# First and sixth Strassen product as one 512-column and one 256-column matmul

## What is computed

```python
def conv_ffn(h, w_up, w_conv, b_conv, w_down):          # first block
    g, v = jnp.split(h @ w_up, 2, axis=-1)              # 1024 -> 2 x 2816
    g = depthwise_conv_seq(g, w_conv, b_conv)           # three taps over the tokens
    return (jax.nn.silu(g) * v) @ w_down
...
proj = h @ w_in[l]                                      # second block, 1024 -> nine parts
xc, gb, gc, q, k, v, g_sw, gate_a, gate_r = jnp.split(proj, split_points, axis=-1)
...
x = x + (jax.nn.silu(h2 @ w_ff_gate[l]) * (h2 @ w_ff_up[l])) @ w_ff_down[l]
```

## Time and profile before

| | us |
|---|---|
| median of 3 runs (1523.29 to 1524.03) | 1523.39 |
| span of the profiled execution, first to last instruction | 1521.2 |
| median over that span | 2.2 |
| PE busy in the span | 1497.1 (98%) |
| DVE busy | 1046.6 (69%) |
| POOL busy | 1013.0 (67%) |
| ACT busy | 635.8 (42%) |

### The profile page before, as it was taken

One profiled execution on the slowest core, in us unless ns is written; L12 is line 12 of the kernel. 1 busy time (PEld: TensorE's weight loads), 2 busy tenths in 40 slices (PEclk: granted clock), 3 DMA queues, 4 the chain that ended last, 5 costly groups with the idle time before them and its releaser, 6 DMA issues.

```text
span 1521.2 us, 26964 instructions
## 1 busy us (share of the span) xinstructions
PE 1497.1 (98%) x9391; PEld 1355.7 (89%) x9391; DVE 1046.6 (69%) x1605; ACT 635.8 (42%) x1142; POOL 1013.0 (67%) x801
## 2 busy tenths in 40 slices
PE   7999999999999999999999999999999999999998
PEld 6998999998887899999888888888888999999897
DVE  7877777873428477766943667676457787777954
ACT  6543566650113355565122213232235565554442
POOL 4735877766666777776764647566466787776684
PEclk9999999999999999999999999999999999999998
DMA  9942333344233333445342232322232333333342
GB/s 374 404 154 73 102 104 97 101 153 160 97 111 87 94 112 116 121 126 152 96 123 69 84 109 83 118 74 83 70 97 84 97 111 103 103 110 87 95 114 69
DMA packets 236382, 179.30 MB, mean 118 GB/s; under 512 B 5393, under 2 KB 214673, under 8 KB 235921
## 3 DMA queue, kind: packets, MB, share of 16 engines
q1 hardware_dynamic: 235008, 171.98, 36.5%
q10 hardware_dynamic: 1296, 6.29, 1.2%
HBM read 173.01 MB, written 5.24 MB: 117 GB/s over the span
## 4 chain that ended last, share of the span: by engine, by line
PE 57%; DVE 5%; issue 3%; POOL 2%; ACT 1%; POOLq 0%; DVEq 0%; ACTq 0%
PE ps L1075 19%; PE ps L1078 19%; PE ps L1079 19%; POOL tmp L929 1%; POOL w_lo L947 0%; POOL tmp L938 0%; POOL rope_r L947 0%; DVE wide_lo L3130 0%; DVE ps L3116 0%; DVE act_lo L3124 0%; DVE ps L3117 0%; DVE ps L3118 0%; DVE tmp L3115 0%; PE ps L1509 0%; DVE gates_r L3124 0%
## 5 line engine op out<-in xcount | busy, mean ns | idle before, releaser
L1075 PE MATMUL ps<-act_hi,w_hi 128*128 128x256 f32 (+1 forms) x864 | 283.6, 328 | 3.0 <-ACT gates L1895 1.3
L915 POOL TENSOR_TENSOR w_lo<-raw,w_hi 128x1024 fp32r<-128x1024 f32 x110 | 274.7, 2497 | 9.2
L1078 PE MATMUL ps<-act_hi,w_lo 128*128 128x256 f32 (+1 forms) x864 | 280.1, 324 | 0.0
L1079 PE MATMUL ps<-act_lo,w_hi 128*128 128x256 f32 (+1 forms) x864 | 280.0, 324 | 0.0
L1075 PE MATMUL ps<-wide_hi,w_hi 128*128 128x512 f32 (+2 forms) x733 | 261.1, 356 | 1.5 <-POOL w_lo L915 0.6
L1078 PE MATMUL ps<-wide_hi,w_lo 128*128 128x512 f32 (+2 forms) x733 | 260.4, 355 | 0.0
L1079 PE MATMUL ps<-wide_lo,w_hi 128*128 128x512 f32 (+2 forms) x733 | 260.4, 355 | 0.0
L912 POOL TENSOR_TENSOR w_hi<-raw,zero 128x1 fp32r<-128x1 f32 x110 | 30.3, 275 | 260.7 <-PE ps L1075 259.8
L947 POOL TENSOR_TENSOR w_lo<-raw,w_hi 128x512 fp32r<-128x512 f32 x128 | 165.8, 1305 | 52.5 <-ACT w_hi L1643 51.9
L1075 PEld LDWEIGHTS ps<-act_hi,w_hi 128*128 128x128 f32 x864 | 165.1, 191 | 19.6 <-issue 3.2
L1078 PEld LDWEIGHTS ps<-act_hi,w_lo 128*128 128x128 f32 x864 | 165.2, 191 | 13.9 <-issue 1.4
(11 more groups left out here) (322 smaller groups left out, 3952.8 us busy)
## 6 DMA issues: line engine op xcount, KB each, us to landing
raw<-in_w_in SPq DMA_DIRECT2D x88, 512.0 KB, 4.2
gates<-in_w_mod_t SPq DMA_DIRECT2D x20, 1024.0 KB, 10.2
raw<-in_w_ffn_up SPq DMA_DIRECT2D x40, 512.0 KB, 3.9
raw<-in_w_ffn_down SPq DMA_DIRECT2D x22, 512.0 KB, 3.6
raw<-in_w_ff_gate SPq DMA_DIRECT2D x22, 512.0 KB, 3.8
raw<-in_w_ff_up SPq DMA_DIRECT2D x22, 512.0 KB, 3.8
raw<-in_w_r_out SPq DMA_DIRECT2D x16, 512.0 KB, 3.4
raw<-in_w_ff_down SPq DMA_DIRECT2D x16, 512.0 KB, 3.8
```

Of the source, the lines that this page charges most:

```text
L915: nc.gpsimd.tensor_tensor(w_lo[:, two, :], raw[:, slot, :], f32(w_hi[:, two, :]), SUB).then_inc(split_done, 1)
L1075: ins = mm(o, w, a, start=start, stop=False)
L1078: mm(o, wl, a, start=False, stop=False)
L1079: return mm(o, w, al, start=False, stop=stop)
```

## The change

F1 and F6 are computed with two matmuls for each of their four feature blocks, in place of three. The first streams 512 columns past the high weights: the 256 columns of the high activations and, from another place of the same tensor, the 256 columns of the low ones. It writes a whole PSUM bank: the high part's result in the low half, the low part's in the high half. The second streams the high activations past the low weights, into the low half. DVE adds the two halves: a new join `q` adds Q1's high half to `part_q1`, `u` then takes Q6's low half, and a new last step takes away Q6's high half. `joined` now counts six steps in a pair (`q`, a step that counts as `p`, `u`, `vw`, `c1`, `c2`), each of the first two followed by a wait of DVE for itself. PE's F1 waits besides for the earlier pair's `q`. High and low activations are laid out as one tensor so that one access pattern reaches both; the sizes are as before.

```diff
--- before.py
+++ after.py
@@ -123,7 +123,7 @@
 HI = {"first": ("copy", F5, F7, F2, F1, F6, F3, F4), "later": ("copy", F1, F6, F7, F5, F2, F3, F4)}
 LO_POOL = {"first": (F7, F2, F5, F1, F4), "later": (F1, F7, F2, F4)}
 LO_DVE = {"first": ("add6", F6, "add3", F3), "later": ("add6", F6, F5, "add3", F3)}
-JOINED = ("u", "vw", "c1", "c2")
+JOINED = ("q", "p", "u", "vw", "c1", "c2")
 
 
 DOWN_PAIRS = 4
@@ -213,7 +213,7 @@
 
 def down_joined(f, j, what):
 
-    at = {"u": 1, "w": 2, "v": 3, "x": 4, "c1": 6, "c2": 8}
+    at = {"u": 1, "w": 2, "v": 3, "x": 4, "c1": 8, "c2": 12}
     return LOADED + (BASE[3 + f] + PAIR * (j - 1)) * len(JOINED) + at[what]
 
 
@@ -257,13 +257,12 @@
         res = sb("res", [P, KT, T])
         with nc.sbuf_tensor("mod_early", [P, KT, D], F32) as mod_early:
             pass
-        act_hi, act_lo = sb("act_hi", [P, KT, T], F32R), sb("act_lo", [P, KT, T], F32R)
-        with nc.sbuf_tensor("wide_hi_plain", [P, FT, T], F32) as wide_hi_plain:
+        act = sb("act", [P, 2, KT, T], F32R)
+        act_hi, act_lo = act[:, 0, :, :], act[:, 1, :, :]
+        with nc.sbuf_tensor("wide_plain", [P, 2, FT, T], F32) as wide_plain:
             pass
-        wide_hi = sb("wide_hi", [P, FT, T], F32R)
-        with nc.sbuf_tensor("wide_lo_plain", [P, FT, T], F32) as wide_lo_plain:
-            pass
-        wide_lo = sb("wide_lo", [P, FT, T], F32R)
+        wide = sb("wide", [P, 2, FT, T], F32R)
+        wide_hi, wide_lo = wide[:, 0, :, :], wide[:, 1, :, :]
         with nc.sbuf_tensor("gates_r", [P, 2 * KT, T], F32R) as gates_r:
             pass
         gates = sb("gates", [P, 2 * KT, T])
@@ -300,7 +299,7 @@
         silu_psum = ps[:, 0:2, :].rearrange("p s t -> p (s t)")
         silu_kept = ((slice(0, REL), decay[:, :]), (slice(REL, D), early[:, 160:160 + D - REL]))
         kept_gates = nc.dram_tensor("kept_gates", (KEPT, P, VT, T), F32, kind="Internal").ap()
-        kept_stage = [w[:, S_KEPT:S_KEPT + PAIR, :] for w in (wide_hi_plain, wide_lo_plain)]
+        kept_stage = [wide_plain[:, i, S_KEPT:S_KEPT + PAIR, :] for i in range(2)]
         identity = tmp[:, 0, 0:P]
 
         identity_late = decay[:, 0:P]
@@ -338,8 +337,12 @@
         def t_view(w, s):
             return w[:, s:s + 6, :].rearrange("p s t -> p (s t)").rearrange("p (k i t) -> p k i t", k=QUAD, i=3)
 
-        t_hi, t_lo = t_view(gates_r, 0), t_view(gates_r, 6)
-        t_hi, t_lo = [t_hi, t_hi, t_view(wide_hi, S_T)], [t_lo, t_lo, t_view(wide_lo, S_T)]
+        def t_view_both(w):
+            return w.rearrange("p j s t -> p j (s t)").rearrange("p j (k i t) -> p j k i t", k=QUAD, i=3)
+
+        t_gates = t_view_both(gates_r[:, 0:12, :].rearrange("p (j s) t -> p j s t", j=2))
+        t_both = [t_gates, t_gates, t_view_both(wide[:, :, S_T:S_T + 6, :])]
+        t_hi, t_lo = ([w[:, i] for w in t_both] for i in range(2))
         T_BANK = [4, 2, 0]
         t_sums = [ps[:, s:s + 2, :].rearrange("p s t -> p (s t)")[:, HALF:4 * HALF].rearrange("p (i t) -> p i t", i=3)
                   for s in T_BANK]
@@ -363,6 +366,12 @@
                 return t1_of(f, k)
             b, t_ = {F1: (k, HALVES[0]), F5: (k, HALVES[1]), F2: (QUAD + k, HALVES[0]), F3: (QUAD + k, HALVES[1])}[form]
             return act_hi[:, b, t_], act_lo[:, b, t_]
+
+        def moving_both(f, form, k):
+
+            if form == F6:
+                return t_both[f][:, :, k, T_AT[f][F6], :]
+            return act[:, :, k, HALVES[0]]
 
         def product_out(form, o):
 
@@ -1078,6 +1087,11 @@
                 mm(o, wl, a, start=False, stop=False)
                 return mm(o, w, al, start=False, stop=stop)
 
+            def half_product(bank, w, wl, both, start, stop):
+
+                mm(ps[:, bank, :], w, both, start=start, stop=False)
+                return mm(ps[:, bank, HALVES[0]], wl, both[:, 0, :], start=False, stop=stop)
+
             def w_block(two, b, n=P):
                 hi, lo = two if isinstance(two, tuple) else (w_hi[:, two, :], w_lo[:, two, :])
                 return hi[:, b * n:(b + 1) * n], lo[:, b * n:(b + 1) * n]
@@ -1234,8 +1248,11 @@
                         if ready:
                             pe.wait_ge(ready[0], ready[1] + k + 1)
                         sl = slice(k * P, (k + 1) * P)
-                        ins = product(product_out(form, p[2]), form_hi(form, p)[:, sl], form_lo(form, p)[:, sl], *moving(f, form, k),
-                                      k == 0, k == QUAD - 1)
+                        w, wl = form_hi(form, p)[:, sl], form_lo(form, p)[:, sl]
+                        if form in (F1, F6):
+                            ins = half_product(1 if form == F1 else 7, w, wl, moving_both(f, form, k), k == 0, k == QUAD - 1)
+                        else:
+                            ins = product(product_out(form, p[2]), w, wl, *moving(f, form, k), k == 0, k == QUAD - 1)
                     ins.then_inc(product_done, 1)
 
                 def bank_free(form, p):
@@ -1257,6 +1274,7 @@
                         pe.wait_ge(t_ready, 2 * QUAD)
                     elif form == F1 and not first:
                         pe.wait_ge(half_copied, LOADED + turn(p))
+                        pe.wait_ge(joined, joined_at(earlier(p), "q"))
                     elif form == F6:
                         pe.wait_ge(joined, joined_at(earlier(p), "u"))
                     elif f == 2 and form in (F7, F2):
@@ -2533,11 +2551,14 @@
 
                 o = p[2]
                 if what == "u":
+                    q1_low, q6, q6_low = ps[:, 1, HALVES[1]], ps[:, 7, HALVES[0]], ps[:, 7, HALVES[1]]
+                    dve.wait_ge(half_copied, LOADED + turn(p) + 1)
+                    tt(part_q1, part_q1, q1_low, ADD).then_inc(joined, 1)
                     dve.wait_ge(product_done, counted(PRODUCTS, p, F6))
-                    dve.wait_ge(half_copied, LOADED + turn(p) + 1)
-                    if not opening(p):
-                        dve.wait_ge(joined, joined_at(earlier(p), "vw"))
-                    ins = tt(part_u, part_q1, product_out(F6, o), SUB)
+                    dve.wait_ge(joined, joined_at(p, "q"))
+                    tt(part_u, part_q1, q6, SUB).then_inc(joined, 1)
+                    dve.wait_ge(joined, joined_at(p, "p"))
+                    ins = tt(part_u, part_u, q6_low, SUB)
                 elif what == "vw":
                     dve.wait_ge(product_done, counted(PRODUCTS, p, F7 if is_first(p) else F5))
                     if not opening(p):
@@ -3154,14 +3175,14 @@
                     if j == 2:
                         dve.wait_ge(part_done, part_at(f, 3))
                     dve.wait_ge(joined, down_joined(f, j, "x"))
-                    tt(ps[:, bank, :], ps[:, bank, :], parts_q1w, ADD).then_inc(joined, 2)
+                    tt(ps[:, bank, :], ps[:, bank, :], parts_q1w, ADD).then_inc(joined, 4)
                 else:
                     dve.wait_ge(product_done, counted(PRODUCTS, p, F4))
                     if j == 2:
                         dve.wait_ge(part_done, part_at(f, 4))
                     dve.wait_ge(joined, down_joined(f, j, "c1"))
                     t_ = slice(0, T) if j < 3 else halves[0]
-                    tt(ps[:, bank + 1, t_], ps[:, bank + 1, t_], tmp[:, 2, t_], ADD).then_inc(joined, 2)
+                    tt(ps[:, bank + 1, t_], ps[:, bank + 1, t_], tmp[:, 2, t_], ADD).then_inc(joined, 4)
 
             def down_dve(f, residual, add):
 
```

## The result

| | before | after |
|---|---|---|
| median of 4 runs each, us | 1523.34 (1523.12 to 1524.03) | 1534.82 (1534.42 to 1535.03) |
| span of the profiled execution | 1521.2 | 1532.7 |

The ratio is 1.0075, 95% interval 1.0062 to 1.0088: the change makes the kernel 11.5 us slower. The prediction said 1531.8, between 1527.5 and 1537, and slower with 0.90. The direction and the place are right, the size is 3.0 us short.

What follows compares the result with a forecast made beforehand. A DVE and ACT ring bounds the first up stage, mostly PE elsewhere. First up stage 8.4, mixing -2.1, second up stage +2.1: +8.4 on span 1521.2, so 1529.6; median 2.2 above, 1531.8 us; range 1527.5 to 1537.

Steps and rivals of the forecast that it cites:

- the ring: First up stage: DVE and ACT wait on each other in a loop of 10.35 us, forecast to grow to 10.92.
- Rival A: First up stage: DVE's idle times absorb the added joins; -2.8 us in all, 1520.6 us; 6%.
- First up stage: Added joins make `vw` later by 0.57 us a period in the ring; the stage costs 8.4 us.
- the 0.31 of slack: First up stage: form F6's low part could start 0.31 us earlier, absorbing that much of the added 0.88.
- PE's saving: F1 and F6 matmuls: 0.107 us less a pair, gaining 2.1 in the mixing stage, 1.8 late in the second up stage.
- rival B: F1 and F6: the two-piece matmul takes 0.240 us and gains nothing; +12.3, 1535.7 us; 13%.
- The case of 1535.0 us: By the skill page's gap PE saves 0.020 us a pair; +11.6, 1535.0 us; counted in rival B's chance.
- the two terms of DVE: Cost of the added joins: 8.4 us in the first up stage, 3.87 at the head of the second up stage.
- Second up stage: +3.9 forecast for its head: Pairs 0 to 4: added joins delay `vw` by 0.35 + 4 x 0.88, so F4 of pair 4 is 3.87 us late.
- rival C: DVE's joins: each link costs more, 1.18 in place of 0.88 us; +5.7 beyond the forecast, 1537.5 us; 10%.
- Rival D: PE's clock falls in its new waits of 0.95 in 10.9 us; would cost tens of us; 1%.

Runs made afterwards that it cites:

- e2b: Changed kernel with the three old 256-column matmuls for F1 and F6 but all three joins (sums not the reference's): 1536.97 us, ratio 1.0090.
- e3: Changed kernel with the new matmuls but the single old join, low activations' half left out of the sums: 1520.66 us, ratio 0.9984.
- e6: Changed kernel, first up stage reordered: joins up to `u` ahead of `add6`, ACT's copy of Q1 ahead of its SiLU: 1526.42 us, ratio 1.0021.
- e7: As e6, with ACT also making form F6's high part ahead of the product's in the first up stage: 1522.78 us, ratio 0.9996.
- e4: Changed kernel with one contiguous 512-column operand for F1 and F6, except each stage's first pair (sums not the reference's): 1535.16 us, ratio 1.0078.
- e11: Changed kernel with F1 and F6 grouped, four 512-column matmuls then four of 256, and contiguous operands (sums not the reference's): 1534.3 us, single run.
- e5: Changed kernel with F1's and F6's matmuls grouped, four of 512 columns then four of 256, same numbers computed: 1534.24 us, ratio 1.0071.
- e1: Changed kernel with the change undone in the first up stage alone: 1525.18 us, ratio 1.0011.
- e10: Changed kernel with one added join instead of two, the last step (taking away Q6's high half) left out: 1526.53 us, ratio 1.0022.

## Why the prediction was right, and where it was short

**What bounds the kernel: right.** Three runs show the ring in the first up stage: the joins alone reproduce its 10.95 (e2b), the matmuls alone leave it at 10.34 (e3), and the same joins in another place give 10.35 back (e6). Rival A, in which DVE's idle times take the joins up, falls: the waits of 1.21 and 0.36 stood unchanged in after. Only joins that are moved into the first of them cost nothing (e6), and it took a second move to bring the ring under PE's pace (e7).

**First up stage: +8.4 forecast, +8.9 measured.** The step from product to `vw` grew by 0.91, not 0.88, as the links are 0.44, 0.46 and 0.45; less the 0.31 of slack that is 10.95, not 10.92, and 0.03 over 13 to 14 pairs makes 0.4 of the 0.5. F4 is held in 13 pairs, and the step to it is 0.93, with about another 0.1 in the step behind: the 0.92 by which DVE's period exceeds PE's 10.03. PE's saving was worth nothing here, as forecast.

**PE's saving: the term that failed.** 0.107 us a pair was forecast and 0.053 is measured, so the mixing stage gives 1.1 and not 2.1, and the later pairs of the second up stage 0.9 and not 1.8: 1.9 of the 3.1 us that the sum was short. The forecast priced a 512-column matmul from a row of 48 alike, 0.227, and this one stands between smaller ones and takes 0.236. The doubt was in the right term and had the wrong cause: rival B blamed the two pieces of the operand, and e4 and e11 show that they cost nothing. The alternation costs 0.02 of the missing 0.054 a pair (e5); the rest is open.

The Trainium skill ("TensorE: Matmul & The Clock Gate", section "Back-to-back issue gap") gives a matmul by itself 2.5 ns beside its columns; 0.020 us a pair is an estimate from that. The trace has 0.053, between that and the forecast, and neither gives the steps of 0.236 and 0.117.

The case of 1535.0 us that the prediction set beside rival B is the nearest to the measured 1534.82, and that is luck: its saving is too small by 0.033 us in each of 37 pairs, 1.2 us, and the two terms of DVE, which it took over, were too small by 0.5 + 0.7, also 1.2.

**Second up stage: +3.9 forecast for its head, +4.6 measured.** `vw` of pairs 0 to 4 is late by another 0.42, 0.98, 1.32, 0.97 and 0.90 us, where 0.35 and four times 0.88 were forecast. That the head is a ring, and that every new step counts in it, was right. Two things are missing. The first is rival C in part. Timeline of DVE, pair 1:

```profile
1193.46 0.70 DVE L2537 TENSOR_TENSOR ps<-ps,raw 128x512 f32<-128x512 f32 x1 [1.21 <-ACT ps L1853]
1194.07 0.41 DVE L2556 TENSOR_TENSOR tmp<-tmp,ps 128x256 f32<-128x256 f32 x1
1194.58 0.42 DVE L2559 TENSOR_TENSOR tmp<-tmp,ps 128x256 f32<-128x256 f32 x1
1195.04 0.42 DVE L2561 TENSOR_TENSOR tmp<-tmp,ps 128x256 f32<-128x256 f32 x1
1195.59 0.69 DVE L2568 TENSOR_TENSOR tmp<-tmp,ps 128x512 f32<-128x512 f32 x1
...
1205.00 0.70 DVE L2537 TENSOR_TENSOR ps<-ps,raw 128x512 f32<-128x512 f32 x1 [0.91 <-ACT ps L1853]
```

The three links are 0.51, 0.46 and 0.55, in all 1.52 for the one of 0.54: +0.98, neither 0.88 nor rival C's 1.18. The forecast priced these pairs with the link of 0.44 from the first up stage, although its own row shows 0.54 in pair 1; two more of that size are 1.08. The order around the step doesn't set this. In after the link from `q` to the next step is 0.44 to 0.45 in every pair that runs in a loop of the program (pairs 7 to 20 of the first up stage, 4 to 19 of the second), and 0.51 to 0.53 in all the others, which are written out one by one, but for 1.01 in one that waited for PE. Pair 20 of the second up stage is written out in the order of the loop, and has 0.51. What makes the difference is not shown.

The second thing is pair 2: its `vw` is late by 0.34 more than its links explain. The last row above is its `add6`, whose `sum_copy` ended at 1203.98 + 0.58 = 1204.56, 0.44 us earlier; that of the period at 303.38 starts 0.12 behind one that ended at 302.68 + 0.58. The late `add6` of pair 2 is in e2b, e4, e5, e6 and e7 too, and isn't in e1, though e1, e6 and e7 differ from after in the first up stage alone; with fewer joins (e3, e10) it isn't there either. Why is open.

**Rival D** fell in after: the clock was granted in full in all three stages. But it isn't empty. PE stands for about 1.9 us ahead of F4 of pair 1 in the second up stage, in after and in e1, e2b, e4, e5, e6, e7 and e11 alike. In six of these eight traces the clock stayed at 2.4 GHz there, and in e1 and e4 it went to 1.2 GHz for a few us behind the wait (granted 0.59 from 1190 to 1193 us in e1, 0.57 from 1198 to 1202 us in e4), where a block of F1 took 0.64 us in place of 0.35. It cost nothing there, as DVE sets the pace: `vw` of pairs 1 to 4 comes at the distances of after, to 0.01 us, in e4. The price of tens of us that the prediction gave D is shown by no run.

**The sum again.** With the measured sizes the same sum closes: 1531.8 + 0.5 (first stage) + 1.9 (PE's saving) + 0.7 (head of the second up stage) = 1534.9, beside 1534.82. The mechanism needed no new term; every term erred to the same side. The measured time lies outside the forecast's own spread of about 2 us; the range held because it reached to B and C, of which the first was about half true in size, and the second a third, in three pairs.

## What to carry to other kernels

Before work is moved onto an engine with idle time, follow who ends that idle time: if it is an engine that itself waits for the first one, the two are a ring, the idle time is a link of it, and an added step lengthens the period by all that goes beyond the slack of its other links (0.31 us here, so 0.22 for one step and 0.60 for two). If the added step can stand where the ring waits anyway, its cost goes (8.6 us here for the same instructions in another order), so the change and its place in the order are to be tried together, and each against the old code in the same new order. Price an instruction from a row in which its neighbours are like those that it will have.

## What the runs showed of the hardware

- A 512-column matmul of fp32r operands takes 0.227 us in a row of its like, 0.236 when it alternates with 256-column ones, and 0.232 in groups of four; a 256-column one takes 0.120 in a row of its like, 0.117 in the alternation and 0.1185 in groups of four. A moving operand in two pieces cost nothing beside a contiguous one.
- A DVE step that needs the 256-column one ahead of it, which lasts 0.41 to 0.42 us, starts 0.44 to 0.56 behind it. In after and before, the same two lines stood 0.44 to 0.46 apart in pairs of a loop and up to 0.51 to 0.56 in pairs written out; in e10 the first of two links took 0.51 to 0.52 in the loop as well. What sets it wasn't found.
- The same wait of PE, about 1.9 us, was followed by a fall of the granted clock to 1.2 GHz in two of eight profiled executions (e1, e4), and by none in the other six.
